# Hybrid encoder layer: another order of the stick-breaking attention's query tiles, and four steps that are tied to it

## The reference

```python
def block(args):                      # SB_BLOCK = 128 queries
    qi, bi = args
    z = jnp.einsum('bhqd,bhkd->bhqk', qi, kf).astype(jnp.float32) * scale
    qpos = bi * SB_BLOCK + jnp.arange(SB_BLOCK)
    before = kpos[None, :] < qpos[:, None]
    log_beta = jax.nn.log_sigmoid(z)
    log_1m = jnp.where(before, jax.nn.log_sigmoid(-z), 0.0)
    tail = lax.cumsum(log_1m, axis=3, reverse=True) - log_1m
    w = jnp.where(before, jnp.exp(log_beta + tail), 0.0)
    return jnp.einsum('bhqk,bhkd->bhqd', w.astype(vf.dtype), vf)
```

## Time and profile before

| | |
|---|---|
| median of 3 runs | 1044.09 us (1043.96 to 1046.66) |
| the profiled execution, its time and span | 1043.6 us, 1041.8 us |
| PE busy | 1017.0 us (98%) |
| DVE busy | 794.2 us (76%) |
| ACT busy | 572.0 us (55%) |
| POOL busy | 88.4 us (8%) |
| mean granted TensorE clock over the span | 0.996 |
| chain that ended last | PE 87%, DVE 5%, ACT 3%, DMA 2% |

### The profile page before, as it was taken

One profiled execution on the slowest core, in us unless ns is written; L12 is line 12 of the kernel. 1 busy time (PEld: TensorE's weight loads), 2 busy tenths in 40 slices (PEclk: granted clock), 3 DMA queues, 4 the chain that ended last, 5 costly groups with the idle time before them and its releaser, 6 DMA issues.

```text
span 1041.8 us, 12454 instructions
## 1 busy us (share of the span) xinstructions
PE 1017.0 (98%) x4982; PEld 820.8 (79%) x4982; DVE 794.2 (76%) x737; ACT 572.0 (55%) x751; POOL 88.4 (8%) x70
## 2 busy tenths in 40 slices
PE   9999999998989999999999999999999999999996
PEld 7878777886757787788788888788888788888784
DVE  6237659698578578877878867998776998777998
ACT  7423432658758536777663557333657333666454
POOL 0013213021312142000000000000000000000000
PEclk9999999999999999999999999999999999999998
DMA  9411111200011544013013022022031031035004
GB/s 341 142 60 41 41 41 41 81 1 1 7 36 42 174 180 173 1 43 119 1 51 111 1 82 81 1 83 78 1 121 41 1 121 41 1 123 201 1 0 162
DMA packets 38657, 74.65 MB, mean 72 GB/s; under 512 B 3236, under 2 KB 12744, under 8 KB 38600
## 3 DMA queue, kind: packets, MB, share of 16 engines
q1 hardware_dynamic: 38456, 73.83, 20.4%
q10 hardware_dynamic: 144, 0.03, 0.0%
HBM read 65.46 MB, written 8.39 MB: 71 GB/s over the span
## 4 chain that ended last, share of the span: by engine, by line
PE 87%; DVE 5%; ACT 3%; DMA 2%; issue 1%; SPq 1%; ACTq 0%; DVEq 0%
PE ps L719 27%; PE ps L723 26%; PE ps L721 26%; PE ps L934 2%; PE ps L888 2%; DMA y<-in_x 2%; PE ps L792 1%; PE ps L959 1%; DVE out_gained L2101 1%; DVE y L2159 1%; DMA xt<-in_x_turned 1%; DVE y L2050 1%; ACT sb_w L1332 1%; PE ps L1036 1%; PE ps L823 1%
## 5 line engine op out<-in xcount | busy, mean ns | idle before, releaser
L719 PE MATMUL ps<-b_op,a_op 128*128 128x512 f32 x448 | 174.6, 390 | 3.6 <-issue 3.6
L719 PE MATMUL ps<-a_op,b_op 128*128 128x512 f32 x448 | 175.4, 392 | 2.5 <-issue 1.4
L723 PE MATMUL ps<-a_op,b_op 128*128 128x512 f32 x448 | 174.4, 389 | 0.0
L721 PE MATMUL ps<-a_op,b_op 128*128 128x512 f32 x448 | 174.3, 389 | 0.0
L723 PE MATMUL ps<-b_op,a_op 128*128 128x512 f32 x448 | 174.3, 389 | 0.0
L721 PE MATMUL ps<-b_op,a_op 128*128 128x512 f32 x448 | 174.3, 389 | 0.0
L1486 ACT CAST a_op<-f 128x1024 fp32r<-128x1024 f32 x56 | 58.8, 1049 | 112.9 <-PE ps L723 72.7
L2007 DVE TENSOR_TENSOR b_op<-wq,b_op 128x1024 fp32r<-128x1024 f32 x96 | 116.9, 1217 | 0.0
L719 PE MATMUL ps<-act_hi,w_hi 128*128 128x512 f32 x288 | 114.6, 398 | 0.8 <-DVE act_lo L1682 0.8
L723 PE MATMUL ps<-act_hi,w_lo 128*128 128x512 f32 x288 | 112.2, 389 | 0.0
L721 PE MATMUL ps<-act_lo,w_hi 128*128 128x512 f32 x288 | 112.1, 389 | 0.0
(11 more groups left out here) (225 smaller groups left out, 1680.7 us busy)
## 6 DMA issues: line engine op xcount, KB each, us to landing
wq<-in_w_ff_in SPq DMA_DIRECT2D x16, 1024.0 KB, 5.4
wq<-in_w_ff_out SPq DMA_DIRECT2D x16, 1024.0 KB, 5.1
stage<-in_w_in SPq DMA_DIRECT2D x16, 512.0 KB, 4.6
y<-in_x SPq DMA_DIRECT2D x4, 1024.0 KB, 13.2
stage<-in_w_out SPq DMA_DIRECT2D x8, 512.0 KB, 3.8
h_spill<-y SPq DMA_DIRECT2D x8, 512.0 KB, 2.7
h_back<-h_spill SPq DMA_DIRECT2D x2, 2048.0 KB, 11.9
out<-y SPq DMA_DIRECT2D x8, 512.0 KB, 2.8
```

The costliest lines, as they stand in the source:

```text
L719: nc.tensor.matmul(dst, stat[0], mov[0], start=first, stop=False, skip_group_check=chained)
L721: nc.tensor.matmul(dst, stat[0], mov[1], start=False, stop=False, skip_group_check=chained)
L723: return nc.tensor.matmul(dst, stat[1], mov[0], start=False, stop=last, skip_group_check=chained)
```

## The change

The query tiles run 7, 6, 5, 4, 0, 1, 2, 3 for the first head pair and 4, 5, 6, 7, 3, 2, 1, 0 for the second. The fills leave units 6 and 7 free in the kernel before and units 4 and 5 in the changed one, so that again the tiles 1 and 0 of each pair go without a fill. `SUM_UNIT` goes from 6 to 5: the window group's sums on PE come behind unit 5. POOL's addition of the squares stays ahead of head 10. DVE's `group_variance(1)` moves from behind head 15 to behind head 12. `MIX_HEADS` goes from (17, 19) to (9, 11), which moves ACT's two round_group steps there and DVE's two rest_group steps from 21 and 23 to 13 and 15. The table preload moves behind the whole loop.

```diff
-        UNITS = [(p, t) for p in range(2) for t in reversed(range(TOK))]
+        UNITS = [(p, t) for p, ts in ((0, (7, 6, 5, 4, 0, 1, 2, 3)), (1, (4, 5, 6, 7, 3, 2, 1, 0)))
+                 for t in ts]
...
-        FILL_UNITS = (0, 1, 2, 3, 4, 5, 8, 9, 10, 11, 12, 13)
+        FILL_UNITS = (0, 1, 2, 3, 6, 7, 8, 9, 10, 11, 12, 13)
         N_EARLY = WINDOW_ROWS + len(FILL_UNITS)
-        SUM_UNIT, SPLIT_HEADS = 6, (7, 21)
-        MIX_HEADS = (17, 19)
+        SUM_UNIT, SPLIT_HEADS = 5, (7, 21)
+        AFTER_SUMS = min(u for u in FILL_UNITS if u > SUM_UNIT)
+        MIX_HEADS = (9, 11)
...
-                if n == 2 * SUM_UNIT - 2:
+                if n == 2 * SUM_UNIT:
                     sum_squares(1, [win_sq[:, 0, :], win_sq[:, 1, :]])
...
-                    if n == row_of(FILL_UNITS[6]):
+                    if n == row_of(AFTER_SUMS):
                         pe.wait_ge(grp_var, 2)
...
-                    pe.wait_ge(row_copied, row_of(FILL_UNITS[6]))
+                    pe.wait_ge(row_copied, row_of(AFTER_SUMS))
                     group_sums(1, 7, win_sq[:, 0, :])
...
-                if n + LEAD == HEADS:
-                    nc.scalar.preload_act_table_set("natural_log_exp_and_others")
+            nc.scalar.preload_act_table_set("natural_log_exp_and_others")
             output_copy(len(UNITS) // CHAIN - 1)
...
-                if a and u == SUM_UNIT + 1:
+                if n == 2 * SUM_UNIT + 2:
                     group_variance(1, 7)
```

## The result

The changed kernel takes 1047.16 us (median of 13 runs, 1046.42 to 1047.70) against 1044.05 us before (13 runs, 1042.75 to 1046.66). The ratio is 1.0025, with a 95% interval of 1.0018 to 1.0033. I had forecast 1041.4 us and a range up to 1043.4.

What follows compares the result with a forecast made beforehand. PE was taken to bound the kernel, so only its waits and lower clock could change. Gone 5.56 us, new 2.9, net 2.66, taken as 2.7: 1044.09 - 2.7 = 1041.4 us, range 1039.6 to 1043.4.

Steps and rivals of the forecast that it cites:

- The bound and the loop: Whole kernel: PE busy 98% of the span; scores(u + 2) waits for sigmoids queued on ACT behind those needing scores(u + 1).
- The three waits of the new valley: Units 4 and 5: PE waits 1.0 at scores(6), 0.75 at head_turn(10), 1.15 at scores(7); 2.9 us in all.
- the walk: Step-by-step timing of ACT, DVE and PE through units 4 and 5 from the end of scores(5); error about 1 us.
- Scores(7): New valley: PE waits 1.15 us for ACT's sigmoids; without the moved round_group, 0.1.
- the round_group that I put ahead of head 13's sigmoids: ACT in the new valley: the moved step adds 1.05 us ahead of scores(7).
- The wide tiles upwards: Units 8 to 11, tiles 4 to 7: ACT's loop 4.7 us against PE's cover of 5.6; spare 0.8, no wait.
- my own signs of being wrong: Brackets in the wide units, over 5 us of waits in the new valley, or a gain at 351 gone at 360.
- the rival in which these units outrun ACT: Units 8 to 11: 1.5 to 2 us too much per loop costs about 6, giving 1047.4 us; chance 0.05.
- The end: Table load behind the loop: weighted(15) waits 0.35, 0.48 us gained; second sums priced 0, at most 0.3.
- The lower clock moves into the new valley: Rival around scores(7): clock falls for 3.4 us, costing 0.5 to 1.7; with 1.4, 1042.8 us; chance 0.22.
- the old valley: Between the head pairs: idle 0.18, 1.28 and 1.12, plus 1.75 us for the lower clock, all forecast to go.
- slower by more: Outcome slower than before by more than the distinguishable 0.3%, 3.1 us; chance 0.05.

Runs made afterwards that it cites:

- no_sums: Changed kernel with the window group's eight one-column sums behind unit 5 replaced by one product; 1043.08 us.
- before_no_sums: Kernel before with the window group's eight one-column sums behind unit 6 replaced by one product; 1044.40 us.
- before_busy: Kernel before with five extra 512-column products of no use in unit 7, ahead of scores(9); 1043.81 us against 1044.51 beside it.
- sums_twice: fill_4_mix with the eight one-column sums behind unit 5 done twice; 1043.88 us.
- mix_early: fill_4_mix with MIX_HEADS at (9, 11) again, late eviction of unit 4's row kept; 1042.64 us.
- fill_4_mix: Changed kernel with unit 3's fill moved to unit 4, ACT's round_group steps back at heads 17 and 19, and unit 4's row evicted later; 1039.86 us.
- busy_waits: Changed kernel with ten extra 512-column products of no use ahead of the three instructions where PE waits in units 4 and 5; 1043.24 us.
- fill_4: Changed kernel with the fill of unit 3 moved to unit 4; 1042.98 us.
- mix_back: Changed kernel with ACT's round_group steps back at heads 17 and 19 and DVE's steps at 21 and 23; 1044.95 us.

## Why the prediction was wrong

**The bound and the loop: right.** PE's queue is the bound, and the loop from scores to sigmoids to scores gives its waits (of the idle times in the earlier trace rows only the 0.43 ends on DVE, the others on ACT). The three waits of the new valley came where the walk put them and summed to 2.55 for 2.9 us. Scores(7) waited 0.65 for 1.15 because its turn and the small weighted ahead of it ran at half clock and covered more; in no_sums, where they ran at full clock, it waited 1.15.

ACT's timeline of after shows the round_group that I put ahead of head 13's sigmoids, as priced (1.17 and 1.05 from start to start; it answers to the earlier trace rows):

```profile
286.55 1.17 ACT L1353 ACTIVATE act_hi<-work,columns_c 128x1024 fp32r<-128x1024 f32 x1
287.60 0.50 ACT L1331 ACTIVATE sb_r<-ps 128x384 f32<-128x384 f32 x1
287.97 0.51 ACT L1335 ACTIVATE sb_w<-ps 128x384 f32<-128x384 f32 x1
```

**The wide tiles upwards: a term put at nothing.** I had spare time of 0.8 us and no wait; there were 0.31 and 0.43 us, ahead of head_turns of units 9 and 10. Those wait for ACT's copies, which I had checked for scores but not for the turns. Brackets in the wide units were among my own signs of being wrong. They cost 0.7 us; the rival in which these units outrun ACT by 1.5 to 2 us each did not happen.

**The end: right.** The wait ahead of weighted(15) is 0.41 for the forecast 0.35 (0.83 before), and from there to group_sums(2) are 8.72 us (363.00 - 354.28) for 8.68 before (359.41 - 350.73). The load costs its 1.28 and no drain, as in the earlier trace rows:

```profile
354.25 1.28 ACT L1402 ACT_TABLE_LOAD   x1
355.54 0.59 ACT L1359 COPY work<-ps 128x512 f32<-128x512 f32 x1
```

So the drain of about 1.38 us that the Trainium skill has on the page "ScalarE: Activation LUTs", section "What ACT_TABLE_LOAD costs", is not seen here either: the next instruction starts 0.01 us behind the load.

**The clock: wrong, and this is the step that failed.** Under "The lower clock moves into the new valley" I had the mechanism as a rival, with a chance of 0.22 and a price of 1.4 us, 1.7 at most. Both were too small. The price rested on one case: in the earlier trace rows the low clock lasts 3.4 us, so I took it to last 3.4 us wherever it falls. There the scores of tile 6, 3.25 us of dense work, run in it, and it comes back. In the new valley it is followed by one narrow scores, turns, one-column sums, turns and a small weighted. It stayed for 13.6 us and came back within scores(8), behind fill 1. Its cost was 5.9 us, not 1.4. (That 1.75 us go from the old valley was right: the ledger has 1.7 there.) It also fell earlier than I had placed it: at 286.35, in the wait ahead of head_turn(10), not at 289 among the sums.

That the length followed from the work behind the fall is my reading and isn't shown: in before_no_sums the same scores(9) follows, and the low clock lasts 10.2 us. What is shown is that one profiled execution gave too short a length even for the kernel before. One of the three runs that I had took 1046.66 us, 2.6 above the median. Seven of the 31 later ones took 1045.7 to 1046.5 at a clock of 0.993, where the profiled one has 0.996, and 0.993 is what before_no_sums has with its 10.2 us. I had that run in front of me and did not ask what it was.

The chance was too small as well, because I counted busy time against busy time and took it as speaking against the fall that the idle time is split up. before_busy and sums_twice show the fall behind 3.4 us in which PE was busy nearly or quite all the time, with turns, one-column sums and small products. And I gave slower by more 0.05, all of it for the wide tiles and none for the clock, which is what made it slower.

With the clock at 1.00 the order itself would have given two thirds of what I forecast. This is an estimate from the ledger: 87.2 us of work and waits of 4.2 (3.70, and the wait ahead of scores(7) 1.15 instead of 0.65) are 91.4 us for the stretch, 1.8 us under the kernel before, where I had 2.7; most of the difference is the 0.31 and 0.43 at the wide tiles. Profile against profile I was 6.3 us out, 1047.2 for 1040.9: 5.9 of clock less the 0.5 of waiting that it covered, and 0.8 to 0.9 on the walk. mix_early and fill_4_mix reach 90.0 and 89.2.

**Which part of the change did it.** The narrow tiles 0 and 1 without fills stand side by side in both orders. In the old one scores(8) and scores(9) of tiles 7 and 6 stand within the valley, 1.99 us and an estimated 1.7 at full clock; in the new one scores of tiles 2 and 3, 0.92 us and 1.13 (the latter in fill_4_mix, at full clock). The sums lie in the valley in both, the round_group steps in the new one only. Taking out the sums (no_sums), filling the waits (busy_waits) or moving a fill (fill_4) each took back 3.9 to 4.2 us of the 5.9 that the clock cost (with no_sums 1.7 of them is the sums' own work), mix_back 2.2. So no part was its single cause, and how much each part adds to the others was not separated.

**What stays open.** Why before's own runs reach from 1041.8 to 1046.5 us is seen in their clocks, but only one execution of each kernel is profiled, so how long the low clock lasted in the others is inferred from their mean clock. Why the clock comes back after 3.4 us in one execution and after 10 in another, behind the same work, is open; the place in the work at which it falls differs from run to run, and no run here sets it. Whether the descending order with a better valley could equal fill_4_mix wasn't tried.

## What to carry to other kernels

When PE is the bound and its work is reordered, list what stands together in the thinnest few microseconds of the new order (those with the fewest scores and 512-column products), waits and small matmuls alike, before adding up waits: the clock's price there (4.3 us) was six times the gain in waits (0.7). Don't take the length of a slow stretch from one fall in one execution: single runs that lie well above the median of the same kernel are a sign that it can be longer. If such a valley can't be filled with work that is due anyway (here one fill moved by one unit, and two steps taken out of ACT's way), put nothing thin behind it; and where single runs of one kernel spread by several microseconds, look at the granted clock of each before explaining a median.

## What the runs showed of the hardware that I had not expected

- The clock fell to 0.50 although PE was busy for 3.33 and for 3.40 of the 3.40 us ahead of it (before_busy and sums_twice). One-column products were 1.84 and some 2.4 us of that.
- Once at 0.50, the clock stayed there for 3.4, 6.8, 10.2 or 13.6 us in the profiled executions, with PE busy most of the time. Each us at 0.50 cost 0.43 to 0.53 us. At 0.50 the sixteen one-column records took 3.41 us for 1.84.
- One program with a valley at the edge took 1041.1 us in one run and 1046.8 in another (mix_back); with the valley filled, the four runs of fill_4_mix lay within 0.14 us.
- Ten products of no use (2.3 us of PE time) made the changed kernel 3.9 us faster (1047.16 to 1043.24, busy_waits).
